# One interleaved block for the rwkv projections and the neighbourhood branch, up to and with its attention

## The reference, cut to what matters

```python
al, bl, cl = jnp.split(pl, [A_PROJ, A_PROJ + B_PROJ], axis=-1)   # pl = hl @ w_in; the same for the context
a_lat, a_ctx  = hgrn2_mixer(ac, al, ...)
b_lat, b_ctx  = rwkv7_mixer(bc, bl, rwkv_mu, ...)
c_lat, c_ctxo = neighbourhood_attention(cc, cl, na_q_gain, na_k_gain, na_rpb, pos_r, pos_c, not last)
xl = xl + g1l * (jnp.concatenate([a_lat, b_lat, c_lat], axis=-1) @ w_out)
```

## Time and profile before

| | us |
|---|---|
| median of 3 runs | 2412.08 (2409.9 to 2414.49) |
| span of the profiled execution | 2420.4 |
| stage rp, within the span | 1250.9 to 1370.7 |
| stage na | 1370.7 to 1486.8 |
| PE busy, of the span | 2190.7 (91%) |
| DVE busy | 901.8 (37%) |
| ACT busy | 511.3 (21%) |
| mean granted TensorE clock | 0.952 |

### The profile page before, as it was taken

The page is one execution under the profiler, slowest core; times in us unless marked ns, Lnnn a source line. Parts: engine busy times, 40 slices in busy tenths (PEclk is TensorE's granted clock), DMA queues, the critical chain, the costliest instruction groups (busy, mean ns, idle before and its releaser), DMA issues. The chain is left out here.

```text
span 2420.4 us, 35520 instructions
## 1 busy us (share of the span) xinstructions
PE 2190.7 (91%) x15188; PEld 1325.0 (55%) x15188; DVE 901.8 (37%) x1861; ACT 511.3 (21%) x1037; POOL 120.5 (5%) x152
## 2 busy tenths in 40 slices
PE   7999999988998999898999887797797899999995
PEld 3445665545776334484785454595595554444442
DVE  3551064425333012148415665645645322111012
ACT  1000162131122001243023254422421110000001
POOL 0000000003320000000000000120120000000001
PEclk9999999999999999999999998997998899999997
DMA  3222201100001951011131000000002899999996
GB/s 134 72 76 78 78 10 36 62 31 27 25 28 40 383 224 62 27 53 44 35 128 44 1 1 20 8 3 20 9 3 87 365 422 425 424 425 424 424 424 247
DMA packets 52716, 328.42 MB, mean 136 GB/s; under 512 B 5968, under 2 KB 10704, under 8 KB 34256
## 3 DMA queue, kind: packets, MB, share of 16 engines
q1 hardware_dynamic: 51408, 321.94, 33.9%
q0 software_dynamic: 1152, 4.19, 0.5%
HBM read 311.43 MB, written 14.68 MB: 135 GB/s over the span
## 5 line engine op out<-in xcount | busy, mean ns | idle before, releaser
L3253 PE MATMUL psum<-m_ring,m_xg 128*64 128x512 f32 x1024 | 229.3, 603 | 15.5 <-issue 14.4
L258 PE MATMUL psum<-h,wring 128*128 128x512 f32 (+1 forms) x448 | 172.6, 535 | 16.8 <-PEq L93 12.4
L525 PE MATMUL psum<-h,wring 128*128 128x512 f32 x384 | 167.7, 600 | 7.2 <-PEq L93 7.2
L3253 PEld LDWEIGHTS psum<-m_ring,m_xg 128*64 128x64 f32 x1024 | 77.7, 139 | 163.9 <-issue 162.6
L258 PEld LDWEIGHTS psum<-h,wring 128*128 128x128 f32 x448 | 84.5, 195 | 83.8 <-issue 73.4
L525 PEld LDWEIGHTS psum<-h,wring 128*128 128x128 f32 x384 | 73.9, 193 | 101.0 <-issue 101.0
L3238 PEld LDWEIGHTS psum<-m_sel,m_htok 128*128 128x128 f32 x1024 | 119.5, 196 | 13.7 <-issue 12.2
L3238 PE MATMUL psum<-m_sel,m_htok 128*128 128x128 f32 x1024 | 123.8, 280 | 1.4 <-DVE m_sel L3229 1.4
L3278 PE MATMUL psum<-m_ring,m_hid_t 128*64 128x512 f32 x512 | 113.4, 595 | 0.7 <-ACT m_hid_t L3381 0.7
L3263 DVE TENSOR_TENSOR m_hid<-rstd,psum 64x512 f32<-64x512 f32 x32 | 22.1, 691 | 229.0 <-ACT rstd L3259 229.0
L2342 PE MATMUL psum<-h,wring 128*128 128x256 f32 (+1 forms) x288 | 98.2, 493 | 1.3 <-PEq L93 1.2
(11 more groups left out here) (573 smaller groups left out, 3566.4 us busy)
## 6 DMA issues: line engine op xcount, KB each, us to landing
m_ring<-in_w_gate SPq DMA_DIRECT2D x32, 2048.0 KB, 25.4
m_ring<-in_w_up SPq DMA_DIRECT2D x32, 2048.0 KB, 27.3
m_ring<-in_w_down SPq DMA_DIRECT2D x64, 1024.0 KB, 25.6
wring<-in_w1f SPq DMA_DIRECT2D x60, 512.0 KB, 3.5
ada_ring<-in_w_ada SPq DMA_DIRECT2D x12, 2048.0 KB, 10.4
wring<-in_w2f SPq DMA_DIRECT2D x31, 512.0 KB, 3.5
expert_rows<-tmp SPq DMA_DIRECT2D x16, 512.0 KB, 26.6
wring<-in_w1v SPq DMA_DIRECT2D x12, 512.0 KB, 3.5
```

Source lines behind the costliest of these rows:

```text
L258: m = nc.tensor.matmul(place(t, out), lhs, rhs, start=(k == 0), stop=(k == KD - 1))
L525: m = nc.tensor.matmul(K.psum[:, banks[t % 4]], ws.weights(first + t, k), h[:, k], start=(k == 0), stop=(k == KD - 1))
L3253: m = nc.tensor.matmul(K.psum[i * SLOTS:(i + 1) * SLOTS, UP + s], W.xg[:, k, s], w[:, k], start=(k == 0), stop=(k == KD - 1))
```

## The change

The stages rp and na become one stage, `rn`. Its first program is the chain tables, norm, rotation, attention (shares 26, 26, 20, 110, in all 182); its second is a chain of the rwkv projections (130 of 182), scales (4), l2 (26) and gates (8). The turning of the values moves into direction 0 of rwkv, ahead of the output projection's first part.

All 8 PSUM banks are to be shared in one stage, so: norm and rotation use banks 0 to 3, the scores 0 to 3, the turns bank 4 alone, the mix bank 5, the projections banks 6 and 7 (one per part of the tokens, no alternation; ACT copies each part by itself), l2 bank 6, gates bank 7. `kk` now lies in `px`. Since l2 uses `K.rstd` while the rotation uses it too, `l2` first waits for all 8 rotated tiles (semaphore `rotated`). In `attention` the points at which the generators yield are moved, and there is a yield before each chunk of the turns.

```diff
@@ attention
-    n_pairs, nseg = len(pairs), len(items[0].segs)
+    n_pairs, nseg, nt = len(pairs), len(items[0].segs), len(tbanks)
...
             for c, (par, j0, n, who) in enumerate(chunks_of[p], first[p]):
                 eng.wait_ge(sem["exped"], 2 * p + par + 1)
-                if c >= 2:
-                    old = flat[c - 2][3]
-                    eng.wait_ge(sem[("copied_act", "copied_dve")[old]], by(old, c - 1))
+                if c >= nt:
+                    old = flat[c - nt][3]
+                    eng.wait_ge(sem[("copied_act", "copied_dve")[old]], by(old, c - nt + 1))
+                yield (p + 1.72 + 0.05 * (c - first[p])) / steps
                 for j in range(n):
-                    m = nc.tensor.transpose(K.psum[:, tbanks[c % 2], j * P:(j + 1) * P],
+                    m = nc.tensor.transpose(K.psum[:, tbanks[c % nt], j * P:(j + 1) * P],
                                             s_sb[:, p % 2, par, (j0 + j) * P:(j0 + j + 1) * P], K.ident[:])
...
-    return attention(nc, K, items, s_sb, pt_sb, stat, take, range(4), range(4, 6), 6)
+    return attention(nc, K, items, s_sb, pt_sb, stat, take, range(4), (4,), 5)
@@ l2, scalar
+            if t == 0:
+                eng.wait_ge(*ready)
@@ rwkv_projections, tensor
-            if t >= 2:
-                eng.wait_ge(sem["emptied"], t - 1)
             for g, (at, n, col) in enumerate(segs):
                 for k in range(KD):
-                    if k % 2 == 0:
+                    if k % 2 == 0 or g == 1:
                         yield (t + (at + n * k / KD) / T2) / nt
-                    m = nc.tensor.matmul(K.psum[:, banks[(t % 2) * 2 + g], :n], ...)
-            m.then_inc(ws.used, 1)
+                    if k == 0 and t >= 1:
+                        eng.wait_ge(sem["emptied"], 2 * t - 1 + g)
+                    m = nc.tensor.matmul(K.psum[:, banks[g], :n], ...)
+                m.then_inc((sem["begun"], ws.used)[g], 1)
@@ rwkv_values replaces rwkv_early
+def rwkv_values(nc, K, p_mix, v_T, bank):
+
     vjobs = [p_mix[:, 4 + m, j * P:(j + 1) * P] for j in range(NCH) for m in range(2)]
+    return turns(nc, K, vjobs, lambda g, ps: nc.vector.tensor_copy(v_T[:, 2 * g:2 * g + 2], ps.rearrange("p (j n) -> p j n", j=2)), [bank], taken=K.v_turned)
@@ second_block
+        kk = px[:, :, 0:T2]
...
+        weave(nc, "rn", in_turn(
+            (26, neighbourhood_tables(nc, K, loads, table, window, none)),
+            (26, rms(nc, K, tiles, lambda t: S if t < 8 else CTX, ..., 1.0 / HD, range(4))),
+            (20, rope(nc, K, tiles[:8], S, cos, sin, range(4), K.rotated)),
+            (110, neighbourhood(nc, K, q, k, v, mix_n, table, none, s_sb, pt_sb, stat))),
+            in_turn((130, rwkv_projections(nc, K, h2, p_mix, px, (6, 7))),
+                    (4, rwkv_scales(nc, K, p_mix, kk)),
+                    (26, l2(nc, K, kk_tiles, lambda t: (S, CTX)[t % 2], [1.0] * 4, 1e-24, [6], (K.rotated, 8))),
+                    (8, rwkv_gates(nc, K, p_mix, up_w, g_T, 7)), over=182), table=LOG_EXP)
...
+        early = lambda d: early_project(nc, K, a, ring, mix_h, mix_n, x1, gain, range(4 * d, 4 * d + 4), (6, 7))
         end = rwkv(nc, K, pr, p_mix, kk, v_T, g_T, up_w, mix_r,
-                   lambda d: early_project(nc, K, a, ring, mix_h, mix_n, x1, gain, range(4 * d, 4 * d + 4), (6, 7)))
+                   lambda d: early(d) if d else in_turn((8, rwkv_values(nc, K, p_mix, v_T, 7)), (60, early(d))))
```

More of the change, by code:

```diff
@@ L598, in values, with rope @@
     return Program(["summed", "emptied"], sync=ws.requests(first, n + nz), tensor=tensor, scalar=scalar)
-def rope(nc, K, tiles, n, cos, sin, banks):
+def rope(nc, K, tiles, n, cos, sin, banks, done):
     nb, nt = len(banks), len(tiles)
@@ L618, in vector @@
             eng.wait_ge(sem["scaled"], t + 1)
-            nc.vector.tensor_tensor(x, x, K.tmp[:, t % 2, :n], ALU.add)
+            nc.vector.tensor_tensor(x, x, K.tmp[:, t % 2, :n], ALU.add).then_inc(done, 1)
     return Program(["rotated", "read", "scaled"], tensor=tensor, vector=vector)
@@ L691, in tensor @@
                 score(p, nseg - 1)
-            yield (p + 0.75) / steps
             if 1 <= p <= n_pairs:
-                turn(p - 1)
+                yield from turn(p - 1)
     def vector(eng, sem):
@@ L728, in vector @@
             if p < n_pairs:
-                mask(p)
-            yield (p + 0.5) / steps
+                yield from mask(p)
+            yield (p + 0.65) / steps
             if 1 <= p <= n_pairs:
@@ L738, in vector @@
                     if who == 1:
+                        yield (p + 0.75 + 0.05 * (c - first[p - 1])) / steps
                         eng.wait_ge(sem["turned"], c + 1)
@@ L1541, in rms, with l2 @@
     return Program(["squared", "summed", "logged", "rooted", "scaled"], scalar=scalar, tensor=tensor, vector=vector)
-def l2(nc, K, tiles, n, gains, floor, banks):
+def l2(nc, K, tiles, n, gains, floor, banks, ready):
     nb, nt = len(banks), len(tiles)
@@ L2347, in scalar @@
         for t in range(nt):
-            yield (t + 1.1) / nt
-            eng.wait_ge(ws.used, first + t + 1)
+            yield (t + 0.4) / nt
             if t >= 2:
@@ L2352, in scalar @@
             for g, (at, n, col) in enumerate(segs):
-                m = nc.scalar.activation(px[:, t % 2, col:col + n], K.psum[:, banks[(t % 2) * 2 + g], :n], ACT.Copy)
-            m.then_inc(sem["emptied"], 1)
+                if g == 1:
+                    yield min(1.0, (t + 1.03) / nt)
+                eng.wait_ge(*((sem["begun"], t + 1), (ws.used, first + t + 1))[g])
+                nc.scalar.activation(px[:, t % 2, col:col + n], K.psum[:, banks[g], :n], ACT.Copy).then_inc(sem["emptied"], 1)
     def vector(eng, sem):
@@ L2407, in rwkv_gates @@
     return Program(["done", "copied"], tensor=tensor, scalar=scalar)
-def rwkv_early(nc, K, p_mix, kk, v_T, g_T, up_w, bank):
-    tiles = [kk[:, m, at:at + n] for m in range(2) for at, n in ((0, S), (S, CTX))]
+def rwkv_values(nc, K, p_mix, v_T, bank):
     vjobs = [p_mix[:, 4 + m, j * P:(j + 1) * P] for j in range(NCH) for m in range(2)]
-    return in_turn(
-        (4, rwkv_scales(nc, K, p_mix, kk)),
-        (26, l2(nc, K, tiles, lambda t: (S, CTX)[t % 2], [1.0] * 4, 1e-24, [bank])),
-        (8, turns(nc, K, vjobs, lambda g, ps: nc.vector.tensor_copy(v_T[:, 2 * g:2 * g + 2], ps.rearrange("p (j n) -> p j n", j=2)), [bank])),
-        (8, rwkv_gates(nc, K, p_mix, up_w, g_T, bank)), over=50)
+    return turns(nc, K, vjobs, lambda g, ps: nc.vector.tensor_copy(v_T[:, 2 * g:2 * g + 2], ps.rearrange("p (j n) -> p j n", j=2)), [bank], taken=K.v_turned)
 def rwkv(nc, K, ph, p_mix, kk, v_T, g_T, up_w, mix, filler):
@@ L2831, in scalar @@
     def scalar(eng, sem):
+        eng.wait_ge(K.v_turned, 3)
         def corner(j):
@@ L3507, in second_block @@
+        kk = px[:, :, 0:T2]
         table, window, none = sb("n_table", [P, 8, 14 * HD], pn), sb("n_window", [P, HD], pn), sb("n_none", [P, CTX], pn)
-        with ExitStack() as p4:
-            px = sb("px", [P, 2, T2 + 3], p4)
-            cos, sin = K.rstd[:, 0], K.rstd[:, 1]
-            loads = [(window[:], a["na_window"]), (table[:], a["na_table"]), (cos, a["cos2"]), (sin, a["sin2"]),
-                     (up_w[:], a["rw_up"]), (K.halves, a["levelc"])]
-            tiles = [q[:, m] for m in range(4)] + [k[:, m, CTX:] for m in range(4)] + [k[:, m, 0:CTX] for m in range(4)]
-            weave(nc, "rp", rwkv_projections(nc, K, h2, p_mix, px, range(4)), in_turn(
-                (26, neighbourhood_tables(nc, K, loads, table, window, none)),
-                (40, rms(nc, K, tiles, lambda t: S if t < 8 else CTX, [K.na_gain[:, 0:1]] * 4 + [K.na_gain[:, 1:2]] * 8, 1.0 / HD, range(4, 8))),
-                (24, rope(nc, K, tiles[:8], S, cos, sin, range(4, 8))), over=100), table=LOG_EXP)
+        s_sb, pt_sb, stat = sb("n_s", [P, 2, 2, 6 * P], pn), sb("n_pt", [P, 2, 6 * P], pn), sb("n_stat", [P, 20], pn)
@@ new lines, in second_block @@
+        cos, sin = K.rstd[:, 0], K.rstd[:, 1]
+        loads = [(window[:], a["na_window"]), (table[:], a["na_table"]), (cos, a["cos2"]), (sin, a["sin2"]),
+                 (up_w[:], a["rw_up"]), (K.halves, a["levelc"])]
+        tiles = [q[:, m] for m in range(4)] + [k[:, m, CTX:] for m in range(4)] + [k[:, m, 0:CTX] for m in range(4)]
+        kk_tiles = [kk[:, m, at:at + n] for m in range(2) for at, n in ((0, S), (S, CTX))]
+        weave(nc, "rn", in_turn(
+            (26, neighbourhood_tables(nc, K, loads, table, window, none)),
+            (26, rms(nc, K, tiles, lambda t: S if t < 8 else CTX, [K.na_gain[:, 0:1]] * 4 + [K.na_gain[:, 1:2]] * 8, 1.0 / HD, range(4))),
+            (20, rope(nc, K, tiles[:8], S, cos, sin, range(4), K.rotated)),
[4 more added lines that the diff above has]
+                    (8, rwkv_gates(nc, K, p_mix, up_w, g_T, 7)), over=182), table=LOG_EXP)
@@ L3518, in second_block @@
         inputs.close()
-        with ExitStack() as p4:
```

(3 more changed lines are left out.)

29 lines of the change are left out of this document (16 added, 13 removed).

## The result

The changed kernel takes 2464.06 us (median of 4 runs, 2457.91 to 2961.62), the kernel before 2410.99 on the same chip: a ratio of 1.0196 [1.0165, 1.0227]. The run of 2961.62 us was in a slower state of the chip and the ratio leaves it out; the other three have a median of 2459.25, 48.3 us more than before. The profiled execution has a span of 2456.1 us. The forecast, 2438 with a range of 2417 to 2454, had the direction, and gave about half of the loss.

The account below looks back on a forecast made before the run. PE was taken as the busiest engine, limited in na by a turned chunk's path through its bank. Six stretches summed to 262.0 us against 235.9, +26.1 us, giving 2438 us, range 2417 to 2454.

Parts of the forecast that it names:

- one bank makes every chunk wait: Turns of a pair: each chunk waits for the copy before, 3.86 us instead of 2.25, so a pair takes 7.57.
- the products stand behind the waits: Between turned chunks: projection products come after the wait, don't fill it, and cover only some 0.4 us per pair elsewhere.
- the stop at the tables: Start of the block: PE has 18.8 us of products, tables end at 28.9, so PE stands 10.1 us.
- norm and rotation: Behind the tables: norm 33.2 us (bounds 27.3 and 38), rotation 21.9 us (bounds 20.5 and 24).
- the handover: Behind the last projected tile: the ninth pair's chunk copy waits behind ACT's mixing wait and table loads, 9.2 us.
- Rival B: One bank costs nothing since ACT and DVE reach copies sooner: 2405 us; chance 0.08 for faster, 0.07 for same.
- Rival C: Projections cover chunk waits where they stand, some 5 us, and the handover costs 3 us: 2427 us, chance 0.23.
- One sign that I gave: Turned chunks start 1.4, 1.0 and 1.4 us apart in every pair, also where a projection stands between.
- Stretch 4: Eight attention pairs beside four projected tiles: 103.0 us, bounds 85 and 108.
- the price of a product in a pair: Projection products on PE: 0.43 us per 256 columns everywhere, 10.26/24, so tiles six to nine give 41.0 us.
- Stretch 6: From the rest of the ninth pair to the next stage, with l2 and gates: 63.9 us, bounds 54 and 80.
- rival A: The clock falls in the eight last pairs, 1.5 to 2 us each: 14 more, 2452 us; chance 0.17.

Follow-up runs that it names:

- the first experiment: The kernel before the change with all four chunks of a pair's turns through one bank, without interleaving: 2466.52 us, ratio 1.0215.
- the split mixing: The changed kernel with two yields between the three steps of each tile's mixing on DVE: 2456.68 us, ratio 1.017 to the kernel before.

## Why the prediction was right or wrong

Right: that one bank makes every chunk wait (1.38 + 1.02 + 1.37 us measured against 3.86; a bare pair at full clock, in the kernel before with one bank, 7.71 against 7.57), that the products stand behind the waits, the stop at the tables (9.9 against 10.1), norm and rotation, and the handover through ACT's order (8.3 against 9.2). The run with two banks shows that without the bank's waits 35.8 of the block's 49.2 us are gone. Rival B is refuted by the first experiment. Rival C's half cover didn't come either: the products covered idle time only once they had been moved ahead of the waits. One sign that I gave didn't fit my own mechanism: chunks 1.4 us apart also where a product stands between. A product behind the wait adds to the wait, and they started 2.27 us apart.

Wrong, the size of two terms:

- Stretch 4, 116.3 instead of 103.0. The step that failed is the price of a product in a pair, 10.26/12 = 0.855 us, taken from rp, where only products and sums of one shape follow each other. In the pair shown it was 4.99 / 5 = 1.0, up to 1.06, since a product between scores and mix adds a switch of the tile shape (0.15 to 0.19 us). With the pair's own part (7.34 against 7.17) that is 0.88 us a pair, 7.0 in eight. The same pace was too low ahead of the first turns: 11.8 us (1331.11 to 1342.93) for 8.5 products and two pairs of scores, 9.9 by my pace, so 2.0 more. Then ACT and DVE being busy when a chunk is due, for which I allowed 2 us: one pair alone lost 4.9 by it (2.64 of stop and the lower clock behind it; the split mixing shows it). And the clock of 0.86 in the eighth pair: 12.28 us with only three products, 1.7 more. 7.0 + 2.0 + 4.9 + 1.7 are 15.6; less the 2 allowed, and 0.4 since the products beside the pairs were 40.6 us and not 41.0, 13.2 of 13.3.
- Stretch 6, 73.4 instead of 63.9: rival A, to which I gave 0.17. The step that failed is that a pair without a filler runs at full clock with PE waiting a third of the time, as in most pairs before. PE did not wait a third of the time there: I took all of 5.96 less 4.1 for waiting, and the pair of the earlier trace rows has stops of 0.56 and 0.19 us only, 13% of its length; the rest is PE's own work, longer than my pace by its switches. Other pairs of before had up to 0.56 and 0.85. With one bank a pair has three stops of 0.6 to 0.8 (in one pair 1.01), 30% of 7.71 us, and the clock fell to 0.83. From 1465.41 to 1505.81 this is 40.4 us where filled gaps made 34.4: 6.0, and with the 0.64 over 9.73 us behind the handover (up to 3.5 more, by the share of time at the lower level) it is the 9.5. The last pairs of this profile, 23.3 us at full clock, took what I had for them (23.7). The kernel before with one bank alone ran most of its pairs at the lower clock in part.

Neither alone explains the time: 2438 with 9.5 for the clock is 2447.5, and only with the 13.3 of stretch 4 is it 2461; the three runs of the ratio have 2459.25.

That median is 48.3 us above before, and the block grew by 49.2, so the runs show no loss outside the block. The stages ahead and behind together took 13.5 us less in this profiled execution than in that of before, which had lain above its median. Direction 0 shows no cost that could be told from this.

## What to carry over

A bank given up by the turns costs twice: once by the copy that each chunk now waits for, and again by the clock, which the small stops can lower; in the kernel before with one bank each part was about half of the loss. Work that is to fill such a wait must stand ahead of it in the engine's order, and is best placed among work of its own tile shape; what each of the two gives was not separated. Only with the second bank kept, and the products in the gaps, did the interleaving gain anything (0.9962).

## What was not expected of the hardware

- Stops of only 0.6 to 0.8 us, three in each pair, held the clock at 0.83 over 40 us; 48 useless transposes in them gave 1.00 and a shorter time. The last pairs of the same profile had the same stops and ran at 1.00 for 23.3 us.
- A change of PE's tile shape between 128x64 and 128x128 costs about 0.15 us at full clock and 0.19 at the lower level. That one to 64x128 costs about as much is read from the spacing of the products (1.06 us against 0.855) and was not tested by itself.
